# One decoder layer with a two-level mixture of experts: expert rows fetched as quarter rows and turned on VectorE instead of TensorE

## What is computed

```python
def hier_moe(x2d, w_rg, w_re, w1, w3, w2):
    lg = x2d @ w_rg;  g_idx = argmax(lg);  p_g = softmax(lg)[g_idx]
    le_sel = (x2d @ w_re)[g_idx]
    top_v, top_i = top_k(le_sel, 2)            # both in the same group
    gate = p_g * softmax(top_v)
    expert = g_idx * 8 + top_i
    # for each expert e, over its tokens:
    #   y = (silu(xb @ w1[e]) * (xb @ w3[e])) @ w2[e]
    return sum over the two experts of gate * y

h = layer_norm(ALPHA * x + mix(x));   y = layer_norm(ALPHA * h + hier_moe(h))
```

## Time and profile before

| | |
|---|---|
| median of 3 runs | 1473.01 us (1471.99 to 1474.28) |
| the profiled execution | 1474.07 us, of which the span of the trace is 1472.2 |
| TensorE busy (PE) | 1309.1 us, 89% of the span |
| VectorE (DVE) / ScalarE (ACT) / GpSimd (POOL) busy | 583.5 / 593.0 / 380.5 us |
| granted TensorE clock, mean over the span | 0.946 of full speed |
| moved by DMA | 261.55 MB, mean 178 GB/s |

### The profile page before, as it was taken

One profiled execution on the slowest core, in us unless ns is written; L12 is line 12 of the kernel. 1 busy time (PEld: TensorE's weight loads), 2 busy tenths in 40 slices (PEclk: granted clock), 3 DMA queues, 4 the chain that ended last, 5 costly groups with the idle time before them and its releaser, 6 DMA issues.

```text
span 1472.2 us, 20676 instructions
## 1 busy us (share of the span) xinstructions
PE 1309.1 (89%) x5827; PEld 649.4 (44%) x5828; DVE 583.5 (40%) x1787; ACT 593.0 (40%) x883; POOL 380.5 (26%) x530
## 2 busy tenths in 40 slices
PE   7949999998999998899999994899999999999800
PEld 3314444666666655345555553333333333333300
DVE  1404343444555555466666555011111111111158
ACT  0000000242445433333333331466666666666445
POOL 5103120000000000355555552122323333333134
PEclk9969999999999999999999996899999999999955
DMA  9423334131122173345554321369899888998684
GB/s 381 155 62 106 114 99 146 54 105 55 54 71 73 58 229 121 113 173 172 180 184 153 119 103 58 119 185 338 225 327 319 279 264 273 344 342 282 192 289 191
DMA packets 83135, 261.55 MB, mean 178 GB/s; under 512 B 15384, under 2 KB 34080, under 8 KB 69894
## 3 DMA queue, kind: packets, MB, share of 16 engines
q1 hardware_dynamic: 62775, 216.26, 40.5%
q0 software_dynamic: 12320, 40.93, 11.8%
q10 hardware_dynamic: 7959, 3.43, 0.9%
HBM read 202.04 MB, written 62.78 MB: 180 GB/s over the span
## 4 chain that ended last, share of the span: by engine, by line
PE 56%; issue 27%; DMA 6%; DVE 3%; ACTq 3%; ACT 2%; POOL 1%; SPq 1%; POOLq 1%; DVEq 0%
PE P L996 11%; PE bank_S L1020 9%; PE P L843 7%; PE M L996 6%; PE bank_S L843 6%; PE bank_S L670 4%; PE P L670 2%; PE bank_T L978 2%; PE M L670 2%; PE bank_T L670 2%; PE M L861 2%; ACTq L1072 2%; DMA const<-in_consts 2%; DMA big<-in_w 1%; DMA work<-conv_rows 1%
## 5 line engine op out<-in xcount | busy, mean ns | idle before, releaser
L996 PE MATMUL P<-big,work 128*64 x416 | 186.9, 603 | 2.7 <-ACT work L1208 2.4
L997 PE MATMUL P<-big,work 128*64 128x512 f32 x416 | 187.1, 603 | 0.0
L709 PE MATMUL P<-big,work 128*128 128x256 f32 (+1 forms) x512 | 173.9, 496 | 0.0
L1236 ACT ACTIVATE big<-big 128x2048 f32 x78 | 144.8, 1903 | 29.4 <-issue 18.7
L1020 PE MATMUL bank_S<-big,work 128*64 x312 | 143.9, 604 | 3.7 <-ACT big L1242 3.1
L1022 PE MATMUL bank_S<-big,work 128*64 128x512 f32 x312 | 143.9, 604 | 0.0
L709 PEld LDWEIGHTS P<-big,work 128*128 128x128 f32 x512 | 97.4, 194 | 70.8 <-issue 64.2
L843 PE MATMUL P<-big,work 128*128 128x512 f32 x256 | 116.2, 608 | 2.7 <-DVE work L1474 2.7
L1689 DVE COPY work<-M 128x256 f32<-128x256 f32 x39 | 16.5, 424 | 253.8 <-PE M L1006 253.8
L843 PE MATMUL bank_S<-big,work 128*128 128x512 f32 x256 | 113.3, 595 | 0.0
L996 PEld LDWEIGHTS P<-big,work 128*64 128x64 f32 x416 | 55.5, 138 | 126.1 <-issue 126.1
(11 more groups left out here) (301 smaller groups left out, 2315.2 us busy)
## 6 DMA issues: line engine op xcount, KB each, us to landing
big<-in_w SPq DMA_DIRECT2D x96, 1024.0 KB, 9.0
work<-in_xt_prompt SPq DMA_DIRECT2D x32, 512.0 KB, 3.7
big<-in_toe SPq DMA_DIRECT2D x16, 512.0 KB, 3.5
work<-in_x_prompt SPq DMA_DIRECT2D x16, 512.0 KB, 4.0
h_rows<-work SPq DMA_DIRECT2D x16, 512.0 KB, 2.7
sum_rows<-work SPq DMA_DIRECT2D x16, 512.0 KB, 3.6
big<-sum_rows SPq DMA_DIRECT2D x16, 512.0 KB, 9.0
out_y_prompt<-big SPq DMA_DIRECT2D x16, 512.0 KB
```

Source lines behind the costliest of these rows:

```text
L709: last = mm(dst[0:n, 0:c1 - c0], lhs[:, k, :], w_qkv[:, k, c0:c1], start=(k == 0), stop=(k == KD - 1))
L996: mm(lower, xgT[:, k, 0:U], both[:, k], start=(k == 0), stop=(k == KD - 1))
L997: last = mm(upper, xgT[:, k, U:P], w_up[:, k], start=(k == 0), stop=(k == KD - 1))
L1236: fn(w_up.rearrange("p k m f -> p m k f")[:, :, ks, :], src, ACT.Copy).then_inc(s[f"wu{part}_ok"], 1)
```

## The change

- The rows are fetched as quarter rows. `h_rows` has the same bytes, seen as rows of 256 values. Each partition of quadrant q (32q to 32q+31) fetches quarter q of a token, in four indirect DMAs per block, one for each group of 32 tokens. Each 32x32 block of `xg` then holds 32 tokens by 32 features that belong in its own quadrant, and one transpose of VectorE (`flip_rows`), which turns blocks of 32x32 in place, gives `xgT`, now three buffers. TensorE's `turn`, ScalarE's `turned` and the wait for `bank_T` go.
- For that each quadrant needs the whole list. A list is fetched as one row of 512 bytes to one partition of each quadrant, and VectorE (`listed`) turns it to one token per partition, computes the numbers of the quarter rows (4 x token + quadrant) and picks each partition's own token and gate for the add. ScalarE asks for the list of block b+6 in block b; SyncE fetches the first six.
- `up` is issued in two halves, and `turn_g(b-1)` stands between the halves of up(b).
- An add waits for the add before last. Two successive blocks hold no token twice, since successive experts are of different groups; the empty slots get four sets of spare rows in place of two.
- VectorE's order becomes turned(b-1), flip_rows(b+1), swiglu(b), listed(b+3), result(b-1).
- In the earlier stages the six semaphores of the small batch's pieces become one that is counted up; the constants get five more columns.

```diff
+        h_pieces, acc_dram, slots_dram, u_dram, conv_dram, at_dram = scratch
+        h_dram = h_pieces.rearrange("(r j) c -> r (j c)", j=4)
...
-        xgT = view(take(D), k=KD, t=P)
+        xgT = [view(take(D), k=KD, t=P) for _ in range(RING)]
...
-        tab = view(sb("tab", 2 * UN)[:, :], j=UN, w=2)
+        lists = take(2 * U * UN)
+        list_cols = view(take(2 * U), w=2, i=2, t=32)
+        pick = view(take(8), w=2, h=2, i=2)
+        own = view(take(2 * UN), j=UN, w=2)
+        piece_idx = view(sb("piece_idx", 4 * RING, I32)[:, :], j=RING, h=2, i=2)
...
-                sp.dma_start(tab[h * U:(h + 1) * U, b], slots_dram[bass.ds(at, U), :]).then_inc(s[f"tab_in{b}"], 16)
+                src = slots_dram[bass.ds(at, U), :].rearrange("(a r) w -> a (r w)", a=1)
+                sp.dma_start(lists[h::32, 2 * U * b:2 * U * (b + 1)], src.broadcast_to([4, 2 * U])).then_inc(s[f"tab_in{b}"], 16)
...
-            sp.wait_ge(s["y_out"], 16 * n_blocks)
+            sp.wait_ge(s["y_out0"], 16 * ((n_blocks + 1) // 2))
+            sp.wait_ge(s["y_out1"], 16 * (n_blocks // 2))
...
-            def turn(b, j, i):
-                pe.wait_ge(s[f"xg_in{j}"], 16 * (i + 1))
-                after(pe, s["xgT_ev"], b - 1)
-                for k in range(KD):
-                    last = tr(T8[:, k, :], xg[j][:, k::KD], ident)
-                last.then_inc(s["pe_xg"], 1)
-
             def weights_at(b):
                 return pe.value_load(block_i[0:1, bass.ds(2 * b + NBT, 1)], min_val=0, max_val=(WR - 1) * WCOLS)
 
-            def up(b, j, i):
+            def up(b, j, part):
                 loaded = pe.value_load(block_i[0:1, bass.ds(2 * b, 1)], min_val=16, max_val=16 * NE)
                 off = weights_at(b)
-                after(pe, s["xgT_ev"], b)
-                for m in range(2):
-                    pe.wait_ge(s[f"w{m}_ld"], loaded)
-                after(pe, s["g_ok"], b - RING)
+                if part == 0:
+                    after(pe, s["xgT_ev"], b)
+                    for m in range(2):
+                        pe.wait_ge(s[f"w{m}_ld"], loaded)
+                    after(pe, s["g_ok"], b - RING)
+                after(pe, s[f"wu{part}_ok"], b)
                 both = wmem[:, bass.ds(off, 2 * KD * FF)].rearrange("p (m k f) -> p k m f", m=2, k=KD)
                 lower, upper = (UP[j][h * U:(h + 1) * U, :].rearrange("p (m f) -> p m f", m=2) for h in range(2))
-                for k in range(KD):
-                    if k % (KD // 2) == 0:
-                        after(pe, s[f"wu{k // (KD // 2)}_ok"], b)
-                    mm(lower, xgT[:, k, 0:U], both[:, k], start=(k == 0), stop=(k == KD - 1))
-                    last = mm(upper, xgT[:, k, U:P], w_up[:, k], start=(k == 0), stop=(k == KD - 1))
-                    if k == KD // 2 - 1:
-                        last.then_inc(s["pe_mid"], 1)
-                last.then_inc(s["pe_up"], 1)
+                for k in range(part * KD // 2, (part + 1) * KD // 2):
+                    mm(lower, xgT[j][:, k, 0:U], both[:, k], start=(k == 0), stop=(k == KD - 1))
+                    last = mm(upper, xgT[j][:, k, U:P], w_up[:, k], start=(k == 0), stop=(k == KD - 1))
+                last.then_inc(s[("pe_mid", "pe_up")[part]], 1)
 
             def turn_g(b):
...
-            turn(0, 0, 0)
             for b in range(RING):
                 up(b, b, 0)
                 if b:
                     turn_g(b - 1)
-                turn(b + 1, (b + 1) % RING, (b + 1) // RING)
+                up(b, b, 1)
                 if b:
                     down(b - 1)
...
-                        up(b, j, i)
+                        up(b, j, 0)
                     with pe.If(b - 1 < n_blocks):
                         turn_g(b - 1)
-                    with pe.If(b + 1 < n_blocks):
-                        turn(b + 1, (j + 1) % RING, i + (j + 1) // RING)
+                    with pe.If(b < n_blocks):
+                        up(b, j, 1)
...
             def slots(b, j6, halves=(0, 1)):
-
+                after(act, s["tab_ok"], b - UN)
                 for h in halves:
                     at = act.value_load(block_i[0:1, bass.ds(2 * b + h + 2 * NBT, 1)], min_val=0, max_val=NE * CAP - U)
-                    act.dma_start(tab[h * U:(h + 1) * U, j6], slots_dram[bass.ds(at, U), :]).then_inc(s[f"tab_in{j6}"], 16)
-
-            def turned(b):
-                after(act, s["pe_xg"], b)
-                after(act, s["pe_up"], b - 1)
-                fn(xgT.rearrange("p k t -> p (k t)"), bank_T[:, :], ACT.Copy).then_inc(s["xgT_ev"], 1)
...
-                after(act, s["y_out"], b - RING, per=16)
-                fn(ye[:, j * D:j * D + 512], bank_S[:, 0:512], ACT.Copy, scale=tab[:, j6, 1:2]).then_inc(s["y_ev0"], 1)
+                if b >= RING:
+                    after(act, s[f"y_out{(b - RING) % 2}"], (b - RING) // 2, per=16)
+                after(act, s["tab_ok"], b)
+                fn(ye[:, j * D:j * D + 512], bank_S[:, 0:512], ACT.Copy, scale=own[:, j6, 1:2]).then_inc(s["y_ev0"], 1)
...
-                if b + RING + 1 < NB:
-                    with where(b + RING + 1):
-                        slots(b + RING + 1, (b + RING + 1) % UN)
+                if b + UN < NB:
+                    with where(b + UN):
+                        slots(b + UN, b % UN)
...
+            def listed(b, j, j6, n, added=None):
+                v.wait_ge(s[f"tab_in{j6}"], 32 * (n + 1))
+                if added is not None:
+                    after(v, s[f"y_out{j6 % 2}"], added, per=16)
+                raw = view(lists[:, 2 * U * j6:2 * U * (j6 + 1)], i=2, t=32, w=2).rearrange("p i t w -> p w i t")
+                nc.vector.transpose(list_cols, raw)
+                v.drain()
+                cols = list_cols[:, :, :, 0:2].rearrange("p w i h -> p w h i")
+                ts(piece_idx[:, j], cols[:, 0], 4.0, C["quarter"], ALU.mult, ALU.add)
+                for w in range(2):
+                    tt(pick[:, w], cols[:, w], C["quad"].rearrange("p (h i) -> p h i", h=2), ALU.mult)
+                v.drain()
+                nc.vector.tensor_reduce(own[:, j6], pick.rearrange("p w h i -> p w (h i)"), AX, ALU.add).then_inc(s["tab_ok"], 1)
+
+            def flip_rows(b, j, n):
+                v.wait_ge(s[f"xg_in{j}"], 64 * (n + 1))
+                after(v, s["pe_up"], b - RING)
+                nc.vector.transpose(xgT[j].rearrange("p k (i t) -> p i k t", i=4),
+                                    xg[j].rearrange("p (i f k) -> p i k f", i=4, k=KD)).then_inc(s["xgT_ev"], 1)
+
...
+            for b in range(RING):
+                listed(b, b, b, 0)
+            flip_rows(0, 0, 0)
             for b in range(UN):
                 if b:
                     turned(b - 1)
+                flip_rows(b + 1, (b + 1) % RING, (b + 1) // RING)
                 swiglu(b, b % RING)
+                listed(b + RING, b % RING, (b + RING) % UN, (b + RING) // UN, (b - RING) // 2 if b >= RING else None)
                 if b:
-                    result(b - 1, (b - 1) % RING, b - 1)
+                    result(b - 1, (b - 1) % RING, b - 1, (b - 1 - RING) // 2 if b > RING else None)
             with v.Fori(1, (NB + UN) // UN) as i:
...
+                    with v.If(b + 1 < n_blocks):
+                        flip_rows(b + 1, (j + 1) % RING, 2 * i + (j + 1) // RING)
                     with v.If(b < n_blocks):
                         swiglu(b, j % RING)
+                    with v.If(b + RING < n_blocks):
+                        listed(b + RING, j % RING, (j + RING) % UN, i + (j + RING) // UN, 3 * i + (j - RING) // 2)
...
-            def gather(b, j, j6, n):
-                hold_ge(s[f"tab_in{j6}"], 32 * (n + 1))
-                hold(s["pe_xg"], b - RING)
-                gcp(idx[:, j6:j6 + 1], tab[:, j6, 0:1]).then_inc(s["idx_ok"], 1)
+            def gather(b, j, j6):
+                hold_ge(s["tab_ok"], b + 1)
+                hold(s["xgT_ev"], b - RING)
+                gcp(idx[:, j6:j6 + 1], own[:, j6, 0:1]).then_inc(s["idx_ok"], 1)
                 hold_ge(s["idx_ok"], b + 1)
-                g.indirect_dma_start(xg[j], None, h_dram,
-                                     bass.IndirectOffsetOnAxis(ap=idx[:, j6:j6 + 1], axis=0)).then_inc(s[f"xg_in{j}"], 16)
-
-            def add_rows(b, j, j6):
+                for i in range(4):
+                    g.indirect_dma_start(xg[j][:, 256 * i:256 * (i + 1)], None, h_pieces,
+                                         bass.IndirectOffsetOnAxis(ap=piece_idx[:, j, i // 2, i % 2:i % 2 + 1], axis=0)
+                                         ).then_inc(s[f"xg_in{j}"], 16)
+
+            def add_rows(b, j, j6, turn):
                 hold(s["y_ev0"], b)
                 hold(s["y_ev1"], b)
-                if not isinstance(b, int) or b:
-                    hold_ge(s["y_out"], 16 * b)
+                if not isinstance(turn, int) or turn:
+                    hold_ge(s[f"y_out{j6 % 2}"], 16 * turn)
```

(8 more changed lines are left out.)

72 lines of the change are left out of this document (39 added, 33 removed).

## The result

The changed kernel took **1463.29 us** (median of 11 runs, 1459.25 to 1469.96) against 1473.05 us of the kernel before, measured beside it (11 runs, 1471.08 to 1480.93): ratio 0.9924, 95% interval 0.9905 to 0.9943. The experiments were measured in three series, each on one chip of its own and with its own runs of the kernel before: series 1 is `regs`, `nest`, `both` and `unsplit`; series 2 is `after2` (the changed kernel again), `all`, `regs_before` and `quarter`; series 3 is `split_before`, `serial`, `twice` and `scal`. In series 2 the changed kernel had a ratio of 0.9973 (0.9952 to 0.9994), so the same kernel can differ by half a per cent, some 7 us, from one series to another, and medians are compared only within a series. The profiled execution took 1459.34 us, of which the span is 1457.5.

The account below looks back on a forecast made before the run. TensorE was taken as the bound, only just, with the DMA engines second. 12.6 + 8.4 - 3.3 = 17.7 us off the profiled 1474.07 gave 1456.4, as a median 1455.3; range 1440 to 1474, leaving out the slower case.

Parts of the forecast that it names:

- DMA takes nearly all: Rival: at 25 ns a packet the later intervals gain nothing; 9 us gained in all, 1464 us; chance 0.15.
- the cover of ScalarE's copy: Expert blocks: ScalarE's second-unit weight copies can start earlier, are wanted 1.3 us earlier, and so stay hidden.
- the tail: End of the kernel, after the expert blocks: claimed to stay as it was, with no term in the sum.
- those for "right": Signs: period near 11.05 before 1100, then uneven; DMA share over 0.93; more weight waits; no list waits; start 3 us later.
- those for "wrong": Signs: TensorE waiting for VectorE's turning; indirect issues over 1.7 us; over 0.6 us from g's transposes to the next product.
- 0.90 us per block off TensorE: Expert blocks: taking the row transposes off TensorE saves 0.90 us each, range 0.6 to 0.95, period about 11.05.
- First 16 intervals: Early expert blocks go at TensorE's pace: 16 x 0.9 less 1.8 for two weight waits, 12.6 us gained.
- Later 21: Later expert blocks are held by the DMA engines' 11.3 us of work: 0.4 us gained each, 8.4 us.
- The evidence for bunches: Weight loads before the change: ScalarE stood eight times until a matrix landed, TensorE once 0.82 us behind that copy.
- Start: Before the first up product: list, three more gather issues and turning make it 3.3 us later, 2 to 6.
- A wait of that size costs nothing: VectorE's queue: gate product and down eviction behind the new waits have 3.3 us of slack and more.
- the slower rival: Rival: GpSimd becomes the bound, first loss at 1.8 us per gather interval; 1492 or 1530 us; chance 0.10.

Follow-up runs that it names:

- regs: Changed kernel with ScalarE fetching the two registers for its second-unit weight copies before its wait for the sigmoid, not after; 1447.53 us, ratio 0.9825.
- nest: Changed kernel with four of the branches per block in VectorE's loop put inside the first, so an empty block costs one; 1455.68 us, ratio 0.9873.
- both: Changed kernel with the edits of `regs` and `nest` together; 1444.38 us, ratio 0.9801.
- unsplit: Changed kernel with turn_g put back behind the whole up product, gathered rows still turned on VectorE; 1469.64 us, ratio 0.9978.
- all: Changed kernel with the edits of `both` and ScalarE's branches nested as well; 1438.71 us, ratio 0.9777.
- regs_before: Kernel before the change with ScalarE's two register loads moved ahead of its wait for the sigmoid's input; 1473.51 us, ratio 1.0003.
- quarter: `both` with only a quarter of w2 loaded for the experts of SyncE's loop, so its output is not the layer's; 1450.98 us, ratio 0.9831.
- split_before: Kernel before the change with turn_g between the halves of the next up product, gathered rows still turned on TensorE; 1485.38 us, ratio 1.0071.
- serial: Changed kernel with each add of rows waiting for the one before it, as before the change; 1469.77 us, ratio 0.9976.
- twice: Changed kernel with VectorE turning the gathered rows twice, the first drained before the second; 1495.54 us, ratio 1.0132.
- scal: `all` without the nesting of VectorE's branches; 1451.59 us, ratio 0.9848.

## Why the prediction came out as it did

The forecast was 1455.3, the result 1463.3: inside the range, at what the rival "DMA takes nearly all" gave (1464), and not by its mechanism. That is in part luck: two terms failed, the cover of ScalarE's copy and the tail. Of the signs named, those for "right" mostly stayed out (plain period 11.3, not 11.05; no share over 0.93; the first product 2.1 us later, not 3), and none of those for "wrong" came either: what went wrong was on no list.

**"These can start earlier ..., so that cover stays": the step that failed.** The copy did start earlier against the sigmoid, by 1.1 us (2.58 to 1.47), not by the 1.96 that its copy and wait measured, since register reads came to light. And it had no slack to begin with: it already ended together with TensorE's own work (11.86 against 11.80). Row 3's junction of 0.46 without idle time looks like TensorE at its own pace, and was a tie; an up product always 2.15 us behind the start of the copy was the sign. I had counted the 0.50 of the two transposes as moved within TensorE's sum, and not as an addition between up and sigmoid.

**0.90 us per block off TensorE**: right to 0.01. With the loop through ScalarE out of the way on both sides it is 11.80 (`regs_before`) to 10.89 (`regs`), 0.91. So close a hit is luck: the new junction took 0.44, not 0.34, and those around the down product 0.42 each, not 0.46. The period stood 0.16 too high in the text (11.05) because a mean over 37 intervals with waits in it, 11.96, was the base. In the changed kernel only 0.54 of it arrived.

**The sum.** First 16 intervals 12.6 forecast, 7.0 measured (191.1 to 184.1), and the failed step is the whole of that: `regs` has 178.5. Later 21: 8.4 forecast, 7.7 measured (251.3 to 243.6), but for the wrong reason. `regs` drove these intervals at 11.10 us, below the 11.3 that I had for the DMA engines' work: its share of 0.96 makes 10.7 us per block, the changed kernel's 0.93 of 11.6 makes 10.8, before had 11.0. The 384 further packets per block don't show. The evidence for bunches was misread, too: of the eight copies that the earlier trace rows puts down to a weight matrix only two (1115.6 and 1271.7) start 0.17 us behind a landing. Start: +3.3 forecast, +2.1 measured, the list taking 1.0 and the turning 2.0; what the sum didn't have is that the last gather of the first block was turned 2.75 us after its issue (919.23 to 921.98), where the one gather before took 4.5 (918.45 to 922.96). Tail: "stays" forecast, +5.4 in the profiled pair. So 17.7 forecast became 14.7 - 2.1 - 5.4 + 0.2 = 7.4 us, plus the variation between runs; the medians say 9.8.

**VectorE.** The turning took 2.04 us, 1.4 forecast, inside 1.1 to 4; its list 1.0 for 1.2. "A wait of that size costs nothing" held for the turning as it stands and not for a doubled one (`twice`), and not for the branches.

```profile
L1695 DVE STREAM_TRANSPOSE work<-work x39: 2007/2040/2049, 922.0 to 1354.1; 128x1024 f32<-128x1024 f32 x39
```

**GpSimd.** Four gathers 1.26 us apart, none over 1.02 us, so the slower rival had nothing to start from:

```profile
L1900 POOL DMA_INDIRECT work<-h_rows,piece_idx x156: 942/953/1019, 915.4 to 1340.9; - x156
```

Nine of the 156 ran beside a turning of VectorE, and took 0.95 us at most; in `twice` 40 did, and took 0.97 at most. So the case of the last rival, issues stretched by VectorE's transposes, didn't arise. The adds landed a little sooner than before, 9.5 us after issue and not 10.9 (line 1909):

```profile
DMA to landing us min/median/max: 6.0/9.5/10.9
```

Wrong: "GpSimd's waits for lists gone"; they are 134.9 us, now for VectorE's making of the list, and cost nothing. The new junction behind the transposes of g is 0.44 us, not 0.34.

## What to carry over

Before you cost a step at nothing because another engine covers it, measure the distance between that engine's step and the one it releases in several blocks: where it is the same each time, the two are tied, and the "cover" is a second bound. Write its loop out term by term, with what the change puts into it.

A removed instruction also hid the sequencer's work beside it. Fetch registers ahead of the wait that they used to share, and nest branches so that an empty turn costs one: these two edits and the third for ScalarE took the kernel from 1470.76 to 1438.71 us in one series (ratio 0.9973 to 0.9777).

## What was not expected of the hardware

- A read of a register from SBUF by ScalarE's sequencer took 0.27 to 0.29 us in most cases and up to 1.44 us; in the changed kernel all long ones (7 of 38) were at one place of the block, and none at the other places.
- An empty turn of VectorE's loop with five branches costs about 1 us (14.9 us of idle time with 14 such turns in it).
- A 128x1024 f32 product of VectorE took 1.28 us alone and 3.39 when GpSimd had begun one 0.04 us sooner; VectorE's last product of the last stage starts at 56 or at 61 to 62.5 us by such meetings.
- 2.99 us of standing still were followed by 6 us at TensorE's lower clock (`twice`, granted 0.50 of full speed). Two stands in `quarter`, 2.79 and 3.36 us long, were not: the granted clock stayed at 1.00.
